# First expert's first three chunks with token rows stationary, the samples' rows gathered ahead of the prompt's, and GpSimd subtracting the low part of the second chunk

## What is computed

```
def expert_choice_ffn(h, w_router, w_gate, w_up, w_down):
    cap = EC_CAPACITY_FACTOR * n_tok // N_EXPERTS          # 128 of the samples, 64 of the prompt
    xt = h.reshape(n_tok, d)
    affinity = jax.nn.softmax((xt @ w_router).astype(jnp.float32), axis=-1)
    g, idx = lax.top_k(affinity.T, cap)
    xe = xt[idx]
    he = jax.nn.silu(jnp.einsum("ecd,edf->ecf", xe, w_gate)) * jnp.einsum("ecd,edf->ecf", xe, w_up)
    ye = (jnp.einsum("ecf,efd->ecd", he, w_down) * g[..., None]).astype(xt.dtype)
    out = jnp.zeros_like(xt).at[idx.reshape(-1)].add(ye.reshape(-1, d))
```

## Time and profile before

| | |
|---|---|
| median of 3 runs | 2579.83 us (2577.54 to 2579.99) |
| the profiled execution | 2577.25 us, its span 2575.5 us |
| mean granted clock of TensorE | 0.994 of full |
| busy: TensorE / VectorE / ScalarE / GpSimd | 98% / 64% / 53% / 10% |
| moved | 503.73 MB, mean 196 GB/s |

### The profile page before, as it was taken

One profiled execution on the slowest core, in us unless ns is written; L12 is line 12 of the kernel. 1 busy time (PEld: TensorE's weight loads), 2 busy tenths in 40 slices (PEclk: granted clock), 3 DMA queues, 4 the chain that ended last, 5 costly groups with the idle time before them and its releaser, 6 DMA issues.

```text
span 2575.5 us, 45337 instructions
## 1 busy us (share of the span) xinstructions
PE 2520.0 (98%) x18610; PEld 2278.5 (88%) x18610; DVE 1649.2 (64%) x1927; ACT 1366.9 (53%) x1559; POOL 266.7 (10%) x238
## 2 busy tenths in 40 slices
PE   8999999999987999999999999999999999999998
PEld 6777777787876999999999999999999999999997
DVE  6555555435387666767666676666767666676667
ACT  6434353424445555555556555555555556555556
POOL 3102020101101010010101101010010101101010
PEclk9999999999997999999999999999999999999999
DMA  4101010135327676676767667676676767667677
GB/s 158 31 17 55 2 55 2 61 122 209 138 96 298 229 253 234 247 252 228 252 228 252 240 241 252 228 252 233 247 252 228 252 228 252 240 241 252 228 253 282
DMA packets 62486, 503.73 MB, mean 196 GB/s; under 512 B 7568, under 2 KB 8080, under 8 KB 37808
## 3 DMA queue, kind: packets, MB, share of 16 engines
q1 hardware_dynamic: 46224, 448.88, 48.0%
q0 software_dynamic: 16160, 53.38, 7.0%
HBM read 465.07 MB, written 37.22 MB: 195 GB/s over the span
## 4 chain that ended last, share of the span: by engine, by line
PE 67%; DVE 1%; ACT 1%; DMA 0%; issue 0%; POOL 0%; POOLq 0%; DVEq 0%; ACTq 0%
PE up_banks_b L2025 15%; PE up_banks_a L2025 15%; PE up_banks_b L2028 6%; PE up_banks_a L2028 6%; PE up_banks_b L2061 2%; PE up_banks_b L2060 2%; PE up_banks_b L2059 2%; PE up_banks_b L2058 2%; PE up_banks_a L2062 2%; PE up_banks_b L2062 2%; PE up_banks_a L2059 2%; PE up_banks_a L2061 2%; PE up_banks_a L2058 2%; PE up_banks_a L2060 2%; PE up_banks_b L2023 1%; PE up_banks_a L2023 1%
## 5 line engine op out<-in xcount | busy, mean ns | idle before, releaser
L1842 DVE TENSOR_TENSOR big_lo<-ew_raw,big_hi 128x4096 fp32r<-128x4096 f32 x192 | 849.6, 4425 | 419.0 <-ACT big_hi L1653 418.9
L1653 ACT CAST big_hi<-ew_raw 128x4096 fp32r<-128x4096 f32 x192 | 697.3, 3632 | 506.5 <-PE up_banks_a L2025 223.7
L2025 PE MATMUL up_banks_b<-x_parts,big_hi 128*128 128x384 f32 x2048 | 582.9, 356 | 0.0
L2025 PE MATMUL up_banks_a<-x_parts,big_hi 128*128 128x384 f32 x2016 | 573.8, 356 | 0.0
L2028 PE MATMUL up_banks_b<-x_parts,big_lo 128*128 128x192 f32 x1792 | 449.0, 251 | 0.0
L2028 PE MATMUL up_banks_a<-x_parts,big_lo 128*128 128x192 f32 x1764 | 442.0, 251 | 0.0
L2025 PEld LDWEIGHTS up_banks_b<-x_parts,big_hi 128*128 128x128 f32 x2048 | 371.0, 189 | 0.0
L2025 PEld LDWEIGHTS up_banks_a<-x_parts,big_hi 128*128 128x128 f32 x2016 | 365.1, 189 | 0.6
L2028 PEld LDWEIGHTS up_banks_b<-x_parts,big_lo 128*128 128x128 f32 x1792 | 341.4, 191 | 0.0
L2028 PEld LDWEIGHTS up_banks_a<-x_parts,big_lo 128*128 128x128 f32 x1764 | 336.1, 191 | 0.6
L64 PE MATMUL bank<-big_hi,w_hi 128*128 128x512 f32 x576 | 236.8, 411 | 0.0
(11 more groups left out here) (320 smaller groups left out, 4076.3 us busy)
## 6 DMA issues: line engine op xcount, KB each, us to landing
ew_raw<-in_expert_weights SPq DMA_DIRECT2D x192, 2048.0 KB, 7.8
w_raw<-in_w_heads SPq DMA_DIRECT2D x48, 256.0 KB, 2.8
x_in<-in_x SPq DMA_DIRECT2D x12, 512.0 KB, 4.4
x_d<-in_x POOLq DMA_DIRECT2D x12, 512.0 KB, 4.1
residual<-x_d POOLq DMA_DIRECT2D x12, 512.0 KB, 2.9
ffn_in<-h_and_xT_d POOLq DMA_DIRECT2D x12, 512.0 KB, 2.9
ew_raw<-residual SPq DMA_DIRECT2D x12, 512.0 KB, 6.7
tab<-in_tables POOLq DMA_DIRECT2D x10, 512.0 KB, 7.6
```

The costliest lines, as they stand in the source:

```text
L1653: nc.scalar.copy(w_hi[:, c % RING], raw[:, c % RAW]).then_inc(hi_done, 1)
L1842: nc.vector.tensor_tensor(w_lo[:, c % RING], raw[:, c % RAW], w_hi[:, c % RING].bitcast(F32), ALU.subtract).then_inc(lo_done, 1)
L2025: last = nc.tensor.matmul(out[:, 0:2 * CAP], hi, x[:, k], start=n == 0, stop=n == KT - 1, skip_group_check=True)
```

## The change

- A class `ExpertStart` holds what both phases share: the routing tables, the identity, the raw buffers (they now lie over w_out's parts), and the semaphores of the weights.
- Chunks 0 and 1 of the first expert are loaded in the output phase, straight to where their low part will lie (`early_raw` lies over `big_lo`), into the columns of samples' tiles already multiplied (chunk 0 when tiles 0 to 3 are, chunk 1 when 4 to 7 are). Chunk 2 is loaded when all tiles are multiplied.
- ScalarE casts them in pieces of 128x1024: chunk 0 in tiles 5 and 6, chunk 1 in tiles 9 and 10. VectorE subtracts chunk 0 in two halves, in tiles 6 and 7. GpSimd subtracts chunk 1 in four pieces in the experts' block, before it gathers the prompt's rows.
- The samples' lists are turned in the output phase behind the last route; their rows are gathered ahead of the store of the last tile's h. Rows lie in `acc` and `h_dram` with the samples first.
- In the experts' block VectorE makes the low parts of the samples' rows behind round 3. TensorE multiplies the samples' part of chunks 0, 1 and (high) 2, with the token rows stationary and 512 weight columns moving, turns both lists between chunks 1 and 2, then does the prompt's part.
- The products of these three chunks lie by token; silu and product are made there, and 12 transposes inside chunk 3 turn them. Chunk 3's and 4's quarters wait for the banks that hold them.
- The first expert's x keeps the low and high parts in another order, so its sums are lowered by two copies each instead of one. Eight transposes that kept TensorE running ahead of the lists (L2069) are gone.

The diff, cut to its core:

```diff
+    def place(self, big, c):
+        first = (c + 1) % self.RING * BLK
+        return big[:, :, first:first + BLK]
+    def load_early(self, sp, c):
+        sp.dma_start(self.place(self.early_raw, c), self.weights[0, c]).then_inc(self.raw_loaded[c], 16)
+    def high_early(self, act, c, tiles):
+        act.wait_ge(self.raw_loaded[c], self.loads(1))
+        return self.nc.scalar.copy(self.hi(c)[:, tiles], self.place(self.early_raw, c)[:, tiles])
+    def low_early(self, eng, on, c, tiles):
+        eng.wait_ge(self.hi_done, c + 1)
+        return on.tensor_tensor(self.lo(c)[:, tiles], self.place(self.early_raw, c)[:, tiles],
+                                            self.hi(c)[:, tiles].bitcast(F32), ALU.subtract)
...
+        WEIGHTS_HIGH = {5: (0, slice(0, 4), False), 6: (0, slice(4, KT), True), 9: (1, slice(0, 4), False), 10: (1, slice(4, KT), True)}
+        WEIGHTS_LOW = {6: slice(0, 4), 7: slice(4, KT)}
...
+                for c in range(ahead.EARLY):
+                    sp.wait_ge(filled, 2 * CH * (c + 1))
+                    ahead.load_early(sp, c)
+                sp.wait_ge(filled, 2 * TT)
+                sp.dma_start(ahead.raw[:, 2], ahead.weights[0, 2]).then_inc(ahead.raw_loaded[2], 16)
...
+                        if t == TT:
+                            pool.wait_ge(h_stored, 16 * (TT - 1))
+                            pool.wait_ge(ahead.tokens_ready, 1)
+                            pool.indirect_dma_start(ahead.xs, None, h_dram[0:SEQS[1][1]],
+                                                    bass.IndirectOffsetOnAxis(token_of[:, 0, 0:1], 0))\
+                                .then_inc(ahead.gathered, 16)
...
                     dve.wait_ge(sum_inv, t + 1)
+                    if t in WEIGHTS_LOW and t == S_TILES - 1:
+                        ahead.low_early(dve, nc.vector, 0, WEIGHTS_LOW[t]).then_inc(ahead.lo_done, 1)
                     first, _, row = LISTS[list_of(t)]
...
+                pool.wait_ge(lo_done, RAW + 1)
+                for k in range(0, KT, 2):
+                    made = ahead.low_early(pool, nc.gpsimd, 1, slice(k, k + 2))
+                made.then_inc(lo_done, 1)
                 pool.wait_ge(tokens_ready, 3)
...
+                rows_are_stored(act)
+                first_x_high(0, S_HI)
+                split(0, 2)
+                sample_silu(0)
+                first_x_high(S_FIRST, P_HI)
+                sample_silu(1)
+                prompt_lower(0)
+                split(0, 3)
+                prompt_silu(0)
+                prompt_lower(1)
+                sample_silu(2)
+                split(0, 4)
+                prompt_silu(1)
+                prompt_lower(2)
+                prompt_silu(2)
+                turned_h_high(0)
...
+                sample_product(0)
+                first_x_low(S_FIRST, P_HI, H_P_LO)
+                dve.wait_ge(lo_done, RAW + 2)
+                split(0, 2)
+                sample_product(1)
+                prompt_sum(0)
+                split(0, 3)
+                prompt_product(0)
+                prompt_sum(1)
+                sample_product(2)
+                prompt_product(1)
+                prompt_sum(2)
+                split(0, 4)
+                prompt_product(2)
+                turned_h_low(0)
...
+                        if first and c == BY_TOKENS:
+                            if f >= 1:
+                                pe.wait_ge(h_made, NTH_SAMPLE[f - 1])
+                        elif first and c == BY_TOKENS + 1:
+                            if f == 0:
+                                pe.wait_ge(p_summed, 1)
+                            else:
+                                pe.wait_ge(h_lo_done, f)
...
+                sample_high(0)
+                sample_low(0)
+                sample_high(1)
+                pe.wait_ge(chosen, 2)
+                for i, lists in enumerate((chosen_gate, chosen_token)):
+                    nc.tensor.transpose(s_bank[0][:, i * ROWS:(i + 1) * ROWS], lists, ident[0:ROWS, 0:ROWS]).then_inc(back, 1)
+                pe.wait_ge(hi_done, BY_TOKENS)
+                sample_high(2)
+                pe.wait_ge(gathered, 32)
+                for r in range(KT // 2):
+                    turn_prompt(r, r).then_inc(turned, 1)
+                pe.wait_ge(lo_done, 2 + RAW)
+                sample_low(1)
+                pe.wait_ge(tokens_ready, 7)
+                pe.wait_ge(turned_lo, 2 * S_FIRST)
+                prompt_both(0)
+                prompt_both(1)
+                pe.wait_ge(lo_done, BY_TOKENS + RAW)
+                sample_low(2)
+                prompt_both(2)
```

More of the change, by code:

```diff
@@ L954, in transform_and_output_phase @@
         pb = lambda n, s: ctx.enter_context(nc.psum_tensor(n, s, F32))
-        table, best, where, token_of, gate_of = routing
+        table, best, where, token_of, gate_of = ahead.routing
+        wo_hi, wo_lo, ident = ahead.wo_hi, ahead.wo_lo, ahead.ident
+        chosen_rows = ahead.chosen_token[0:NE]
         uT, even, m, folded, FOLD = fourier.u, fourier.even, fourier.m, fourier.folded, fourier.FOLD
@@ L1159, in _ @@
                     head_high(LATE_HEADS.get(t, ()))
+                    if t in WEIGHTS_HIGH:
+                        c, tiles, last = WEIGHTS_HIGH[t]
+                        for k in range(tiles.start, tiles.stop, 2):
+                            made = ahead.high_early(act, c, slice(k, k + 2))
+                        if last:
+                            made.then_inc(ahead.hi_done, 1)
                     act.wait_ge(added, 2 * t + 2)
@@ L1644, in body @@
                     pool.sem_inc(rows_free, 1)
-                experts(pool, body)
+                experts(pool, body, first=0)
             @block.scalar
@@ L1917, in h_low @@
                         last.then_inc(h_lo_done, 1)
[L1919 removed]
+                    for c in range(first_chunk, CHUNKS):
                         if c == UPS:
@@ L2008, in up_chunk, with sample_high, sample_low @@
-                def up_chunk(e, c):
+                def sample_high(c):
+                    for k in range(KT):
+                        nc.tensor.matmul(sample_bank[c], x[:, k, S_HI], ahead.hi(c)[:, k], start=k == 0, stop=False)
+                        nc.tensor.matmul(sample_bank[c], x[:, k, H_S_LO], ahead.hi(c)[:, k], start=False, stop=False)
+                def sample_low(c):
+                    for k in range(KT):
+                        last = nc.tensor.matmul(sample_bank[c], x[:, k, S_HI], ahead.lo(c)[:, k], start=False, stop=k == KT - 1)
+                    last.then_inc(sample_made, 1)
@@ new lines, in prompt_both, with turn_h @@
+                def prompt_both(c):
+                    for k in range(KT):
+                        nc.tensor.matmul(prompt_bank[c], x[:, k, H_P_BOTH], ahead.hi(c)[:, k], start=k == 0, stop=False)
+                        last = nc.tensor.matmul(prompt_bank[c], x[:, k, H_P_BOTH], ahead.lo(c)[:, k], start=False, stop=k == KT - 1)
+                    last.then_inc(chunk_done, 1)
+                def turn_h(c):
+                    pe.wait_ge(h_made, max(NTH_SAMPLE[c], NTH_PROMPT[c]))
+                    for i in range(2):
+                        part = slice(i * P, (i + 1) * P)
+                        nc.tensor.transpose(h_bank[c][:, i, S_HI], sample_h[c][:, part], ident[:])
+                        last = nc.tensor.transpose(h_bank[c][:, i, P_HI], prompt_h[c][:, part], ident[0:CAP_P, 0:CAP_P])
+                    last.then_inc(h_turned, 1)
@@ L2031, in up_chunk @@
                             last.then_inc(gates_done, 1)
-                    last.then_inc(chunk_done, 1)
+                        if first and c == BY_TOKENS and f >= 1:
+                            if f == 3:
+                                last.then_inc(chunk_done, 1)
+                            turn_h(f - 1)
+                    if not (first and c == BY_TOKENS):
+                        last.then_inc(chunk_done, 1)
                 def last_down_chunk(e, c, i, part):
```

335 lines of the change are left out of this document (190 added, 145 removed).

## The result

| | before | after |
|---|---|---|
| median | 2579.91 us (2577.54 to 2580.81, 4 runs) | 2600.72 us (2599.86 to 2602.57, 4 runs) |
| ratio | 1 | 1.0083 (95%: 1.0066 to 1.0101) |
| profiled execution, its span | 2577.25, 2575.5 us | 2602.57, 2600.8 us |
| mean granted clock | 0.994 | 0.995 |

What follows compares the result with a forecast made beforehand. TensorE, busy 98% of the span, bounds the kernel, with gaps only at the hand-over. From a mean of 2578.65, less 4.6 gained, plus 1.7 for one fall of the clock: 2575.8 us; range 2570.0 to 2581.0.

Steps and rivals of the forecast that it cites:

- D: Hand-over: VectorE's rounds hold up GpSimd's subtraction, making the prompt's gather late; 2586 at 7 us a piece; chance 0.08.
- Tile 7: Output phase: VectorE's half subtraction ahead of the affinities has no cover, costing 2.2; TensorE idles 2.65.
- one fall: TensorE's clock drops to half speed after one of two new waits, costing 1.7; even odds for each.
- The samples' rows: Hand-over: gather issued at 778.2, behind the last tile's h; rows land 5.1 later, at 783.3.
- TensorE starts: Hand-over: first matmul with the samples' rows at 788.6, set by VectorE's low parts; gather has 2 us of cover.
- The low clock at TensorE's start: Samples' part: some 3.8 us of TensorE's work go at half speed and cost 1.9.
- The lists: Between chunks 1 and 2: TensorE reaches them at 799.5, ready by 795.8, so the written order sets their turning.
- GpSimd: Experts' block: four subtractions of chunk 1, 2.9 to 3.0 each, 783.4 to 795.4; 5 us of cover, cost 0.
- The prompt's rows: Hand-over: rows land at 804.9, while TensorE works on the third chunk's samples until 803.4; 1.5 idle.
- The 12 transposes: Behind the hand-over: turning the first three chunks' products takes TensorE 1.5 at full clock.
- The wait in chunk 4: Fourth quarter: TensorE stands still 2.4 until VectorE has made the third turned piece's low part; bounds 0 and 3.5.
- The fill: Filling TensorE's idle time at the hand-over ends chunk 4 at 842.0 instead of 846.65, gain 4.6.

Runs made afterwards that it cites:

- a_pad224: Kernel after with 224 bytes of padding behind next_token, so wo_hi, tab, x_parts and h_parts lie at 128 modulo 256 again; 2576.09 us, 0.9990.
- a224_low6: a_pad224 with the second half of chunk 0's subtraction on VectorE moved from tile 7 to tile 6, behind its h; 2573.48 us, 0.9982.
- a224_dve1: a_pad224 with chunk 1's subtraction done by VectorE in one instruction instead of GpSimd's four pieces; 2583.29 us, 1.0017.
- a224_warm: a224_low6 with twenty short transposes keeping TensorE busy while it waits for the gathered and rounded rows; 2571.28 us, 0.9969.
- b_all32: Kernel before with 32 bytes of padding ahead of big_hi, so all operands move together; 2579.45 us, one run.
- b_all128: Kernel before with 128 bytes of padding ahead of big_hi, so all operands move together; 2580.22 us, one run.
- a_pad32: Kernel after with one more 32-byte buffer behind next_token; 2594.76 us, 1.0061 of the kernel before.
- a_pad96: Kernel after with 96 bytes of padding behind next_token; 2605.31 us, 1.0103 of the kernel before.
- b_x32: Kernel before with 32 bytes ahead of x_parts and 224 behind it, so only x_parts changes its remainder; 2583.36 us, one run.
- b_h32: Kernel before with 32 bytes ahead of h_parts, moving it and what lies behind it; 2595.61 us, one run.

## Why the prediction was wrong

**The step that failed** is in the first part: "So the whole change can be read at one point: when is chunk 4 of the first expert done ... Whatever is gained or lost there stays, since the 187 chunks behind it are unchanged." Their instructions are unchanged, their operands' addresses are not, and each expert lost 1.54 us. The same step hides in the rivals: all of them, D too, are mechanisms of the hand-over, with its 2586 as the worst. None could give 2600, and the chance of 0.09 for slower held none for this.

With the addresses restored (a_pad224) the median is 2576.09 against a predicted 2575.8. That the sum comes out close is partly luck, since two terms in it are off and cancel. By its steps:

- **Tile 7**: forecast a wait of 2.65, found 2.62. That it was on the path is shown by a224_low6. The clock did fall behind it: from 726 to 729 the granted clock of the kernel after is 0.50, and a224_low6 gives the 2.2 and 1.4 more back. The forecast of one fall, 1.7, held here; by the five traces with this wait (four falls) the chance of it should have been above even odds. The other wait that the forecast counted for the clock, 2.4 in chunk 4, came as 0.91, and the granted clock is 1.00 from 844 to 849.
- **The samples' rows**: h begins at 782.34 where it began at 774.51: 7.8 later, of which 3.7 is the later stretch (720.54 against 716.80), 2.4 the forecast and 1.7 the low clock. The gather is issued 2.2 behind that (forecast 1.3; by the trace it waited for the token copy behind h), and the rows land 5.4 later (forecast 5.1).
- **TensorE starts**: forecast 788.6, found 794.56. Of the 6.0, 3.7 is the later stretch and 1.7 the low clock; 0.5 is left. Most of it is VectorE's, as forecast the last: its rounds in this block begin at 788.34, 0.4 later than 782.5 and the 5.4 give, and end at 792.84. The 2 us of cover for the gather were used up all the same: the gather's chain was 1.2 late as above, and ScalarE's first cast came 2.5 after the rows had landed, since it waited for the store of h, too. VectorE stood still for 0.15 for it. ScalarE and VectorE in the kernel after:

```profile
792.52 0.65 ACT L1856 CAST x_parts<-up_banks_a 128x256 fp32r<-128x256 f32 x2 [7.98 <-DMA ffn_in<-h_and_xT_d]
```

```profile
793.00 0.76 DVE L2021 TENSOR_TENSOR x_parts<-up_banks_a,x_parts 128x256 fp32r<-128x256 f32 x2 [0.15 <-ACT x_parts L1856]
```

- **The low clock at TensorE's start**: the forecast's 3.8 at half speed, cost 1.9, is what passes in the kernel before from its transposes at 791.52 to the full clock at 795.3. In the kernel after the granted clock is 0.50 from 777.2 to 797.7, so 3.1 of the work begun at 794.56 go at half speed, 1.6 by the halved speed; in a_pad224 it is 5.0 and in a224_low6 5.2. The 40 matmuls to the lists, 0.233 apart at full clock where the forecast had 0.226, make up the 0.3 that is left.
- **The lists** were turned when TensorE reached them, 10.92 after its start (forecast 10.9): the order written down sets it, as forecast.
- **GpSimd**: four pieces took 9.41, 2.35 each for the forecast 2.9; they began late, behind the store of h, and still ended (802.03) before the gather was wanted (806.3). Rival D did not occur: no piece took over 2.41 beside VectorE's rounds.
- **VectorE beside GpSimd**: VectorE's copy at 799.97 took 2.11, where it took 0.19 in the kernel before, and ended at 802.08, when GpSimd's last piece had (802.03). It cost nothing, since TensorE turned the lists 1.9 us after the merge was done. The instructions of VectorE's rounds beside the pieces took no longer than before (0.42 for MAX8). An issue of a gather took 4.54 and 5.14 (a224_dve1) beside a subtraction of VectorE's, where one took 1.02 beside the rounds and 1.01 at 806.74 in the kernel after: in these cases an instruction of one of the two engines took longer beside one of the other, and why is not shown.
- **The prompt's rows**: forecast 1.5 idle, found 0.55: the third chunk's last matmul starts at 809.33 and has its 0.23, the transposes start at 810.11.
- **The 12 transposes**: mis-sized. Forecast 1.5 together, from eight at half clock in 1.97 (granted 0.50 from 791 to 795). TensorE in the kernel after:

```profile
837.05 0.33 PE L2178 MATMUL up_banks_a<-ident_e,h_space 128*128 128x128 f32 x1
837.31 0.27 PE L2179 MATMUL up_banks_a<-ident_e,h_space 64*128 64x64 f32 x1
837.51 0.45 PE L2207 MATMUL up_banks_a<-x_parts,big_hi 128*128 128x384 f32 x1
```

  They follow each other by 0.20 to 0.27 at full clock, and chunk 3, from 825.53 to 837.51, took 11.98: 2.8 above its 9.16. That is as much as the eight took at half clock (1.97, 0.25 each). Halving the price with the clock is not wrong by itself: the transposes of one tile in a224_warm go from 0.213 to 0.110. The error was to take the price of eight equal ones for these, which alternate between 128x128 and 64x64 and read another tile each time; which of it makes them dear is not shown.
- **The wait in chunk 4**: forecast 2.4, found 0.91. TensorE came to it later by the 1.3 that the transposes took more, so it waited that much less: the two errors cancel.

**The fill.** The forecast had 2.9 gained up to chunk 4 (4.6 less 1.7); the traces have 2.2 (after) and 2.3 (a_pad224), and the medians 2.3 (by the interval of the ratio, 0 to 5).

## What to carry to other kernels

When a change adds, removes or reorders buffers, even one of 8 bytes, the start addresses of TensorE's operands belong to the diff (32 bytes ahead of `wo_hi` alone made 1.0087 of the kernel before, b_shift32): compare them modulo 256, stationary against moving, before reading anything into the time, and pad until the pairs that agreed agree again. When a kernel bound by TensorE gets slower, compare the distance of the same matmuls in the two traces far from the change before looking for a wait. And where an engine's idle time is to be filled, ask which other engine the filling will hold up: filling VectorE's idle 4 us cost 5.4 (a224_dve1).

## What the hardware showed that I had not expected

The distance of fp32r matmuls that follow each other without a wait went, in these kernels, with where their operands start relative to each other (remainders modulo 256 bytes within the partition; wo_hi is as tab; the last column is the mean distance of the 128x512 matmuls of the output phase from 600 to 700, pauses left out):

| kernel | big_hi | tab | x_parts | h_parts | up chunk, us | down matmul, us | output-phase matmul, us |
|---|---|---|---|---|---|---|---|
| before, a_pad224 | 128 | 128 | 128 | 128 | 9.093 | 0.2275 | 0.2278, 0.2277 |
| b_all32 | 160 | 160 | 160 | 160 | 9.093 | 0.2275 | 0.2277 |
| b_all128 | 0 | 0 | 0 | 0 | 9.093 | 0.2275 | 0.2276 |
| after, b_shift32 | 128 | 160 | 160 | 160 | 9.160 | 0.2338 | 0.2332 |
| a_pad32 | 128 | 192 | 192 | 192 | 9.107 | 0.2338 | 0.2290 |
| a_pad96 | 128 | 0 | 0 | 0 | 9.200 | 0.2333 | 0.2324 |
| b_x32 | 128 | 128 | 160 | 128 | 9.160 | 0.2275 | 0.2278 |
| b_h32 | 128 | 128 | 128 | 160 | 9.120 | 0.2338 | 0.2278 |

Equal remainders have the short distances at all three places tried (128, 160 and 0); a difference of 32, 64 or 128 bytes costs 0.2 to 1.2% of an up chunk, 2.6 to 2.8% of a down matmul and 0.6 to 2.4% of an output-phase matmul (least at 64: 0.2290, beyond the 0.2276 to 0.2278 at equal remainders). The up chunk of b_h32, whose own operands agree, stands outside this. Differences below 32 and between 128 and 256 were not tried. That whole steps of 256 change nothing is seen on `x_parts`: at 175488 (before) and at 186496 (a_pad224), 43 x 256 further, the up chunk takes 9.093. The distance of the same matmuls goes from 0.2275 to 0.2338 with the places alone (b_shift32); what in the chip does it, and whether the reads of the two operands get in each other's way, is not shown. The measurement decides.
